# mLSTM heads of a hybrid recurrent decoder step: rows fetched one head ahead, exponents before the weight parts, own semaphores for three signals

## The chip, the cores and the metric

The kernel runs on one core of one Trainium2 chip. The metric is the device time of one execution in microseconds (us). The engines are named as in the profile: PE (TensorE), PEld (its weight loads), DVE (VectorE), ACT (ScalarE), POOL (GpSimd), SP (SyncE). SP and ACT issue the transfers (DMAs).

## The reference, cut to what matters

One step of a two-layer trunk runs for a prompt of 512 tokens and for 8 sampled sequences of 4 tokens each, with shared float32 weights. A layer is a SwiGLU block, a mixing block of three branches, and a second SwiGLU block. The change lies in the first two branches of the mixing block, of four heads each. Branch A is an mLSTM; per chunk:

```python
b = jnp.cumsum(fc, axis=-1)
D = jnp.where(causal, b[..., :, None] - b[..., None, :] + ic[..., None, :], -jnp.inf)
m_inter = b + m[..., None]
m_t = jnp.maximum(m_inter, jnp.max(D, axis=-1))
s_inter = jnp.exp(m_inter - m_t)
w = jnp.einsum('bhtd,bhsd->bhts', qc, kc) * jnp.exp(D - m_t[..., None])
num = jnp.einsum('bhts,bhsv->bhtv', w, vc) + s_inter[..., None] * jnp.einsum('bhvd,bhtd->bhtv', C, qc)
den = jnp.sum(w, axis=-1) + s_inter * jnp.einsum('bhd,bhtd->bht', n, qc)
h = num / jnp.maximum(jnp.abs(den), jnp.exp(-m_t))[..., None]
C_new = decay[..., None, None] * C + jnp.einsum('bhsv,bhsd->bhvd', vc * wk[..., None], kc)
```

The head's output goes through a layer norm and a gate. Branch B is a gated linear attention (GLA): `o = A v + (q exp(b)) S`, with a decay of each key dimension, an RMS norm and a gate. All final states are outputs too.

## The kernel before

The 544 tokens are the columns of every activation, features are the partitions. The prompt's chunks in the heads are 128 tokens long, four of them (`C`, `NC`); the 32 sample tokens are the columns from `T` on.

**The stream of weights.** Every projection is a sequence of blocks of weights, 1 MB each. SP loads a block into one of two halves of `stage` (`load`, L308) as soon as the block before in that half is split. A float32 weight is used in two parts: ACT writes the high part `wh` (`split_hi`, L729), DVE the rest `wl` (`split_lo`, L1002), and PE multiplies in three passes (`three_pass`, L379). A block gives two tiles of output, one in each pair of PSUM banks (`stream_a`, `stream_b`). DVE takes a tile out of PSUM (`take`, L992), which frees the pair. Every engine runs its own program in order, and semaphores tie them together: `split_done`, `hi_done`, `tile_done` and `tile_free` count blocks and tiles, others are those of a step.

**An mLSTM head** has four blocks and eight tiles: q (t), k (t+1), the values with tokens as rows (t+2 of the prompt, t+3 of the samples), two tiles of each of two gates (t+4 to t+7). Between them stands the head's own work, in four PSUM banks `mix` (`Q`). On PE (L505): q and k, values, then the scores and the transposed keys (L517 to L525, signal `a_scores`), tile t+4, the four updates of the state (`updates`, L535, which wait for `a_kw`), most of tile t+5, sample outputs, the outputs over the chunks (L553), tile t+6, the column sums of the mean (L573, wait for `a_h`, matmuls at L502), sample updates (L495), tile t+7, the column sums of the squares.

On ACT (L824) a head begins with the fetch of its row of four vectors of 544 numbers, spread over all partitions, out of a scratch tensor in DRAM (`RB`, L829). It then waits for it, makes `SI` and `EM` by exponentials (L832), waits for the stored states of the head before, loads `CS` and `nS`, makes two high parts, waits for `a_exin` from DVE and makes the exponents `Ex` (L842). Further on come the gates' sigmoids and `head_root`, a square root that ends the norm and for which GLA's next head waits (`root_done`, matmuls at L596).

On DVE (L1230): take q and k, split n+2, `qs`, take the values, among them `four_parts` of `V4` (L1157), split n+3, the two adds into `Ex` (L1249, L1252), signal `a_exin`, wait for `a_ex` and `a_scores`, then `wS`, `wSs`, `Kw` (the weighted keys for `updates`), `w1`, `Kf`, and `masked_keys` (L1170: four parts `K4`, then `Kws`, the operand of the sample updates), whose end is the one signal `a_kw`. Then `qn`, take t+4, the four states `Cst`, the merge of the head before, and so on. The denominators, the output `Hh`, its sum `wS` (L1294, signal `a_h`) follow the take of t+5 and split n+4.

Head 0 of a layer is a copy with `first=True`: its values are taken first, and the columns `cols` come out of PSUM before `a_exin`. Before it, `gate_rows` (L1106) builds the rows. On PE and DVE heads 1 to 3 are one loop; on ACT all four heads are.

**A GLA head** (PE L588, ACT L861, DVE L1309) has the same blocks. Its wait `b_took` of 10 releases its updates (L636); DVE signals it after `masked_keys`. Behind the states come the merge of the head before, take t+6, the copy out of `mix` (L1392), a square sum (L1210, signal `b_sqs`, which PE awaits at L657) and take t+7.

Of the kernel before, what the change touches and what calls it, by code (L numbers as in the profile page):

```python
# [23 lines left out]
ALU = mybir.AluOpType  # L24
ACT = mybir.ActivationFunctionType
ds = bass.ds
# [94 lines left out]
def trunk(nc, x_T, w_up1, w_down1, w_mix, w_gates, w_o, w_up2, w_down2, vec, b_if, w_lr2, w_ra, w_ri, consts, level_masks,  # L121
          m0, c0, n0, s0, h0, conv0, o_y, o_pc, o_pm, o_ps, o_ph, o_pconv,
          o_sc, o_sn, o_sm, o_ss, o_sh, o_sconv, rows_dram):
    with ExitStack() as ctx:
# [141 lines left out]
        a_mean, a_hc, a_sq, a_sqs = sem("a_mean"), sem("a_centred"), sem("a_squares"), sem("a_square_sum")  # L266
        a_var = sem("a_var")

        b_lr, b_cs = sem("b_lr_loaded"), sem("b_state_loaded")
# [108 lines left out]
        def _(pe):  # L378
# [126 lines left out]
            def mlstm_head(L, i, first=False):  # L505
# [20 lines left out]
                if first:  # L526
                    pe.wait_ge(rows_ready, L + 1)
                    for c in range(NC + 1):
                        row = merged[0:HEADS, 3, :]
                        m = C if c < NC else NS  # L530
                        mm = pe.matmul(Q[0:m, 2, 200 + c * HEADS:200 + (c + 1) * HEADS], row[:, c * C:c * C + m],
                                       ident[0:HEADS, 0:HEADS], start=True, stop=True)
# [40 lines left out]
                def mean():  # L573
                    pe.wait_ge(a_h, B + 1)
                    column_sum(wS, 0, a_mean)
                    sample_updates(0, 2, a_us)

# [10 lines left out]
            def gla_head(L, i):  # L588
# [49 lines left out]
                def outputs():  # L638
                    pe.wait_ge(b_c, B * NC + NC)
                    pe.wait_ge(b_cs, B * 16 + 16)  # L640
                    for v in range(2):
                        pe.matmul(Q[:, 2, v * NS:(v + 1) * NS], val[:, NC, v * P:(v + 1) * P], wSs[:],
                                  start=True, stop=False, skip_group_check=True)
                        sample_states(2, v, v * NS, lambda s_, v_: CS[:, s_, v_ * P:(v_ + 1) * P])
                    for v in range(2):
                        vs = slice(v * P, (v + 1) * P)
                        for c in range(NC):
                            sl = slice(c * C, (c + 1) * C)
                            mm = pe.matmul(Q[:, v, sl], val[:, c, vs], wS[:, sl], start=True, stop=c == 0)  # L649
                            if c:  # L650
                                mm = pe.matmul(Q[:, v, sl], Cst[:, c - 1, vs], qs[:, sl], start=False, stop=True)
                    mm.then_inc(b_out, 1)
                    sample_updates(0, 3, b_us)

# [62 lines left out]
        def _(act):  # L717
# [105 lines left out]

            def mlstm_head(L, i):  # L824
                B = L * HEADS + i
                nh = L * (LAYER_BLOCKS // 2) + i * (HEAD_BLOCKS // 2) + BLK_MIX // 2
                t = L * LAYER_TILES + i * HEAD_TILES + (TILE_MIX + GATE_TILES)
                stored = L * (16 * STORES) + i * 48 + 32
                act.dma_start(RB.rearrange("p a b -> p (a b)"),  # L829
                              spread(rows_dram[ds(i, 1), :], 0, P)).then_inc(a_rows, 16)  # L830
                act.wait_ge(a_rows, B * 16 + 16)
# [4 lines left out]
                act.dma_start(nS[:, 0, :], n0[L, i]).then_inc(a_cs, 16)  # L836
                split_hi(nh + 1, 0, t + 1, 2 * D)
                split_hi(nh + 1, 1, t + 3, 2 * D)
                act.wait_ge(a_exin, B + 1)
                for c in range(NC):  # L840
                    sl = slice(c * C, (c + 1) * C)
                    act.activation(Ex[:, sl], Ex[:, sl], ACT.Exp, bias=cols[:, ds(i + c * HEADS, 1)])  # L842
                act.activation(Ex[0:NS, T:N], Ex[0:NS, T:N], ACT.Exp,
                               bias=cols[0:NS, ds(i + NC * HEADS, 1)]).then_inc(a_ex, 1)
                gates = gate_tiles(t + 4)
                next(gates)
# [89 lines left out]
            def mix(L):  # L936
# [9 lines left out]
                act.dma_start(lr2[64:80, :], w_lr2[L, 0]).then_inc(b_lr, 16)  # L946
                with act.Fori(0, HEADS) as i:
                    mlstm_head(L, i)
                with act.Fori(0, HEADS - 1) as i:
                    gla_head(L, i)  # L950
# [32 lines left out]
        def _(dve):  # L983
# [122 lines left out]
            def gate_rows(L):  # L1106
# [11 lines left out]
                link(dve.tensor_tensor_scan(R[5], reset[0:HEADS, :], R[7], 0.0, ALU.mult, ALU.add))  # L1118
                link(tt_(R[3], R[4], R[5], ALU.subtract))
                take(L * LAYER_TILES + (TILE_MIX + GATE_TILES), 0, qT[:])  # L1120
# [31 lines left out]
            def take_sample_values(t):  # L1152
                tile_ready(t)
                v_ = val[0:NS, NC, 0:DV]
                ts_(v_, pair[1][C - NS:C, 0, 0:DV], rstdT[C - NS:C, NC:NC + 1], None, ALU.mult).then_inc(tile_free, 1)
                dve.wait_ge(tile_free, t + 3)
                four_parts(V4, v_, (0, 1), (2, 3))  # L1157

# [9 lines left out]
            def masked_keys(src):  # L1168

                four_parts(K4, src, (0, 2), (1, 3))  # L1170
                return tt_(Kws[:], spread(K4[:].bitcast(F32).unsqueeze(1), 1, SEQS), spread(seqm[:].unsqueeze(2), 2, P),
# [58 lines left out]
            def mlstm_head(L, i, first=False):  # L1230
# [7 lines left out]
                if not first:  # L1238
                    take(t, 0, qT[:])
                    take(t + 1, 1, kT[:], DK ** -0.5)  # L1240
                    split_lo(n + 2, 0, 2 * D)
                if first:
                    take_values(t + 2)
                dve.wait_ge(a_si, B + 1)
                link(tt_(qs[:], qT[:], SI, ALU.mult))
                if not first:
                    take_values(t + 2)
                split_lo(n + 3, 1, 2 * D)
                link(tt_(Ex[:, 0:T].rearrange("p (c t) -> p c t", c=NC),  # L1249
# [3 lines left out]
                if first:  # L1253
# [3 lines left out]
                    ins = dve.tensor_copy(cols[:, 0:NC * HEADS], Q[:, 2, 200:200 + NC * HEADS])  # L1257
                ins.then_inc(a_exin, 1)
                dve.wait_ge(a_ex, B + 1)
                dve.wait_ge(a_scores, B + 1)  # L1260
# [4 lines left out]
                link(tt_(wSs[0:NS], Ex[0:NS, T:N], Q[0:NS, 2, 0:NS], ALU.mult))  # L1265
                link(tt_(Kw[:], Q[:, 1, :].rearrange("p (c t) -> p c t", c=NC),
                         spread(exv[:, :, C - 1:C], 2, P), ALU.mult))
                link(dve.tensor_reduce(w1[0:NS], Ex[0:NS, T + TS - 1:N:TS], mybir.AxisListType.X, ALU.add))
                link(ts_(Kf[0:NS], Q[0:NS, 2, NS:NS + P], w1[0:NS], None, ALU.mult))
                masked_keys(Kf[0:NS]).then_inc(a_kw, 1)  # L1270


# [4 lines left out]
                for c in range(NC):  # L1277
                    states(c, DV + P, lambda c: SI[:, c * C + C - 1:(c + 1) * C], lambda c: c, a_u, a_c, B * NC)
                if not first:
                    merge_head(i - 1, True, number - 1)  # L1280
# [28 lines left out]
            def gla_head(L, i, first=False):  # L1309
# [72 lines left out]
                for e in range(NLS):  # L1382
                    link(dve.copy_predicated(As, masks[0:NS, NL - NLS + e, 0:NS], Q[0:NS, 1, (e + 1) * NS:(e + 2) * NS]))
                masked_keys(Q[0:NS, 1, P:2 * P]).then_inc(b_took, 1)
                take_gate(L, i, t + 5, 1, 1, acts + 1, "silu", None)
                split_lo(n + 4, 0, 2 * D)
                for c in range(NC):
                    states(c, DV, lambda c_: eb[:, c_ * C + C - 1:(c_ + 1) * C], lambda c_: c_, b_u, b_c, B * NC)
                merge_head(HEADS - 1 if first else i - 1, first, number - 1)
                take_gate(L, i, t + 6, 0, 0, acts + 2, "branch", gcol)  # L1390
# [277 lines left out]
```

## Time and profile before

| | us |
|---|---|
| median of 3 runs (range) | 3363.17 (3357.52 to 3373.01) |
| the profiled execution | 3364.34 |
| its span, first to last instruction | 3362.5 |
| PE busy in the span | 3217.6 |
| DVE busy | 1929.6 |
| ACT busy | 1011.5 |
| mean granted clock of TensorE | 0.972 of full speed |

Busy times are sums over all instructions of an engine. A row of a timeline gives the start and length of a group of like instructions that follow each other, and in brackets how long the engine idled before it and for whom. Rows of the window view give the granted clock as a share of full speed, which is 2.4 GHz; 0.50 is 1.2 GHz. Heads 0, 1, 2 and 3 of the first layer's mLSTM do their updates at 481.9, 556.7, 630.6 and 704.5 us of the span.

### The profile page before, as it was taken

What the parts mean: (1) busy time and instruction counts of PE and PEld (TensorE: products, weight loads), DVE (VectorE), ACT (ScalarE), POOL (GpSimd) and SP (SyncE); (2) the same over time, 40 slices, a digit from 0 to 9 for tenths busy, and PEclk for the clock granted to TensorE, in tenths of its full rate; (3) what the DMA queues carried; (4) which work ended last, traced back from release to release, by engine and by line L of the source; (5) the groups of instructions that cost most, each with busy time, mean ns of one, the idle gap of its engine ahead of it and who ended that gap; (6) DMA issues with size and microseconds to landing.
All of it is one profiled execution on the core that took longest, in us unless ns stands there. A gap on an engine that the chain in (4) does not pass through costs nothing.

```text
span 3362.5 us, 58957 instructions
## 1 busy us (share of the span) xinstructions
PE 3217.6 (96%) x24852; PEld 3163.4 (94%) x24852; DVE 1929.6 (57%) x2645; ACT 1011.5 (30%) x961; POOL 7.4 (0%) x24
## 2 busy tenths in 40 slices
PE   7999989999999999999999999899999999999997
PEld 7999989989999989999999999899899999899997
DVE  5434556657777875434454345555677778754344
ACT  3222222223332653212232123222333246432122
POOL 0000000000000000000000000000000000000000
PEclk9999989999999999999999999899999999999999
DMA  3222222232222222222222222133222222222222
GB/s 140 78 103 83 80 87 94 90 118 87 77 89 72 82 77 88 78 97 83 80 89 83 97 80 95 66 129 115 77 77 83 83 75 83 73 90 83 92 82 68
DMA packets 51744, 294.43 MB, mean 88 GB/s; under 512 B 9224, under 2 KB 12040, under 8 KB 22712
## 3 DMA queue, kind: packets, MB, share of 16 engines
q1 hardware_dynamic: 37440, 243.60, 21.2%
q10 hardware_dynamic: 13696, 48.54, 3.9%
q8 instruction: 68, 1.11, 0.1%
q0 software_dynamic: 512, 0.94, 0.1%
q14 instruction: 28, 0.23, 0.0%
HBM read 271.56 MB, written 21.50 MB: 87 GB/s over the span
## 4 chain that ended last, share of the span: by engine, by line
PE 75%; DVE 14%; ACT 6%; issue 4%; DMA 1%; ACTq 0%; DVEq 0%; SPq 0%
PE stream_b L383 33%; PE stream_a L383 29%; PE stream_a L457 5%; PE mix L487 2%; ACT wh L733 2%; DVE wl L1005 2%; PE mix L538 1%; DVE xc L1432 1%; PE mix L649 1%; PE mix L558 1%; DVE seven L1351 1%; DVE wS L1371 1%; ACT L919 1%; DVE tg L996 1%; PE stream_b L457 1%
## 5 line engine op out<-in xcount | busy, mean ns | idle before, releaser
L733 ACT ACTIVATE wh<-stage 128x2048 fp32r<-128x2048 f32 (+2 forms) x246 | 435.9, 1773 | 819.2 <-PE stream_b L383 586.9
L1005 DVE TENSOR_TENSOR wl<-stage,wh 128x2048 fp32r<-128x2048 f32 (+2 forms) x248 | 525.8, 2120 | 171.3 <-ACT wh L733 154.1
L383 PE MATMUL stream_a<-xh,wh 128*128 128x272 f32 x2560 | 545.6, 295 | 30.2 <-DVE wl L1005 16.1
L383 PE MATMUL stream_b<-xh,wh 128*128 128x272 f32 x2560 | 537.1, 291 | 9.3 <-DVE lyg L996 7.0
L383 PE MATMUL stream_a<-xh,wl 128*128 128x272 f32 x2560 | 536.4, 291 | 0.0
L383 PE MATMUL stream_a<-xl,wh 128*128 128x272 f32 x2560 | 535.0, 291 | 0.0
L383 PE MATMUL stream_b<-xh,wl 128*128 128x272 f32 x2560 | 528.5, 288 | 0.0
L383 PE MATMUL stream_b<-xl,wh 128*128 128x272 f32 x2560 | 528.1, 288 | 0.0
L383 PEld LDWEIGHTS stream_a<-xh,wh 128*128 128x128 f32 x2560 | 410.1, 192 | 37.6 <-issue 22.8
L383 PEld LDWEIGHTS stream_b<-xh,wh 128*128 128x128 f32 x2560 | 402.8, 188 | 15.1 <-DVE lyg L996 7.8
L383 PEld LDWEIGHTS stream_a<-xh,wl 128*128 128x128 f32 x2560 | 411.0, 192 | 0.0
L383 PEld LDWEIGHTS stream_a<-xl,wh 128*128 128x128 f32 x2560 | 407.8, 192 | 0.0
L383 PEld LDWEIGHTS stream_b<-xh,wl 128*128 128x128 f32 x2560 | 402.4, 189 | 0.0
L383 PEld LDWEIGHTS stream_b<-xl,wh 128*128 128x128 f32 x2560 | 400.3, 189 | 0.0
L996 DVE TENSOR_TENSOR us<-stream_b,rstd 128x544 f32<-128x544 f32 x88 | 63.8, 725 | 446.1 <-PE stream_b L383 445.9
L784 ACT ACTIVATE sg<-gs 128x544 f32<-128x544 f32 x88 | 58.0, 659 | 398.7 <-DVE gs L996 398.7
L457 PE MATMUL stream_a<-wh,xh 128*128 128x256 f32 x512 | 146.6, 286 | 6.1 <-DVE qT L996 6.1
L457 PE MATMUL stream_a<-wh,xl 128*128 128x256 f32 x512 | 147.2, 287 | 0.0
L383 PE MATMUL stream_b<-hh,wh 128*128 128x272 f32 x704 | 146.0, 289 | 0.0
L383 PE MATMUL stream_a<-hh,wh 128*128 128x272 f32 x704 | 146.0, 289 | 0.0
L457 PE MATMUL stream_a<-wl,xh 128*128 128x256 f32 x512 | 145.9, 285 | 0.0
L383 PE MATMUL stream_a<-hh,wl 128*128 128x272 f32 x704 | 145.3, 287 | 0.0
(325 smaller groups left out, 4684.9 us busy)
## 6 DMA issues: line engine op xcount, KB each, us to landing
stage<-in_w_up SPq DMA_DIRECT2D x88, 1024.0 KB, 4.8
stage<-in_w_mix SPq DMA_DIRECT2D x88, 1024.0 KB, 4.8
stage<-in_w_down SPq DMA_DIRECT2D x32, 768.0 KB, 4.2
stage<-in_w_down SPq DMA_DIRECT2D x32, 640.0 KB, 3.8
seven<-rows_scratch ACTq DMA_DIRECT2D x8, 1088.0 KB, 8.2
CS<-in_c ACTq DMA_DIRECT2D x8, 1024.0 KB, 4.7
out_o_sc<-CS ACTq DMA_DIRECT2D x8, 1024.0 KB
CS<-in_s ACTq DMA_DIRECT2D x8, 1024.0 KB, 4.8
```

The lines of the kernel that those rows point to most:

```text
L383: mm = [pe.matmul(out(h), a(h), b(h), start=f, stop=z) for h in range(2)]
L457: mm = pe.matmul(out, a[:, k, tok:tok + C], b[:, j, k * DV:(k + 1) * DV], start=f, stop=z)
L487: mm = pe.matmul(Q[:, b_, out_col + s_ * TS:out_col + (s_ + 1) * TS], lhs_of(s_, v), qs[:, T + s_ * TS:T + (s_ + 1) * TS], start=False, st ...
L538: pe.matmul(Q[:, c, 0:DV + P], Kw[:, c, :], val[:, c, :], start=True, stop=True).then_inc(a_u, 1)
L558: mm = pe.matmul(Q[:, v, sl], val[:, c, vs], wS[:, sl], start=True, stop=c == 0)
L649: mm = pe.matmul(Q[:, v, sl], val[:, c, vs], wS[:, sl], start=True, stop=c == 0)
L733: act.activation(wh[:, slot, 0:width], stage[:, slot, 0:width], ACT.Copy).then_inc(hi_done, 1)
L784: act.activation(sg[:], gs[:], ACT.Silu).then_inc(silu_done, 1)
L919: act.activation(lyg[:, v, :], lyg[:, v, :], ACT.Gelu_apprx_tanh).then_inc(l_act, 1)
L996: ins = tt_(halves(dst), banks(pair[slot]), rs2, ALU.mult)
L1005: tt_(wl[:, slot, 0:width], stage[:, slot, 0:width], wh[:, slot, 0:width].bitcast(F32), ALU.subtract).then_inc(split_done, 1)
L1351: tt_(ev[:, :, a, :], ev[:, :, a, :], sv[:, :, a, :], ALU.mult)
```

## The change

It has six parts. ACT fetches the rows of a head while the head before runs, behind that head's exponents (`load_rows`), and only the three rows in use. ACT's exponents of `Ex` stand ahead of the two high parts in heads 1 to 3; in head 0 between them; the heads of ACT are one copy for head 0, a loop of two, and one for head 3. DVE's adds into `Ex` stand right behind the take of k; split n+3 moves behind the states. `Kw` becomes the last step before `a_kw`; `masked_keys`, which now includes V4's parts, comes behind it and has its own signal `a_keys`. In GLA `masked_keys` moves behind the states, with a copy of the keys in its old place and a signal `b_keys` of its own. The wait in front of L531 is for a signal after row R[3] rather than for all rows.

```diff
@@ PE @@
                 if first:
-                    pe.wait_ge(rows_ready, L + 1)
+                    pe.wait_ge(a_row, L + 1)
...
                     column_sum(wS, 0, a_mean)
+                    pe.wait_ge(a_keys, B + 1)
                     sample_updates(0, 2, a_us)
...
                     mm.then_inc(b_out, 1)
+                    pe.wait_ge(b_keys, B + 1)
                     sample_updates(0, 3, b_us)
@@ ACT @@
+            def load_rows(i):
+                act.dma_start(RB[:, 0:3, :].rearrange("p a b -> p (a b)"),
+                              spread(rows_dram[ds(i, 1), 0:3 * N], 0, P)).then_inc(a_rows, 16)
...
-                act.dma_start(RB.rearrange("p a b -> p (a b)"),
-                              spread(rows_dram[ds(i, 1), :], 0, P)).then_inc(a_rows, 16)
                 act.wait_ge(a_rows, B * 16 + 16)
...
-                split_hi(nh + 1, 0, t + 1, 2 * D)
-                split_hi(nh + 1, 1, t + 3, 2 * D)
+                if first:
+                    split_hi(nh + 1, 0, t + 1, 2 * D)
                 act.wait_ge(a_exin, B + 1)
...
+                if not first:
+                    split_hi(nh + 1, 0, t + 1, 2 * D)
+                if not last:
+                    act.wait_ge(a_ex, B + 1)
+                    load_rows(i + 1)
+                split_hi(nh + 1, 1, t + 3, 2 * D)
                 gates = gate_tiles(t + 4)
...
-                with act.Fori(0, HEADS) as i:
+                load_rows(0)
+                mlstm_head(L, 0, first=True)
+                with act.Fori(1, HEADS - 1) as i:
                     mlstm_head(L, i)
+                mlstm_head(L, HEADS - 1, last=True)
@@ DVE @@
-                link(tt_(R[3], R[4], R[5], ALU.subtract))
+                tt_(R[3], R[4], R[5], ALU.subtract).then_inc(a_row, 1)
+                dve.wait_ge(a_row, L + 1)
...
                 dve.wait_ge(tile_free, t + 3)
-                four_parts(V4, v_, (0, 1), (2, 3))
...
+                four_parts(V4, val[0:NS, NC, 0:DV], (0, 1), (2, 3))
                 four_parts(K4, src, (0, 2), (1, 3))
...
                     take(t + 1, 1, kT[:], DK ** -0.5)
-                    split_lo(n + 2, 0, 2 * D)
...
                 dve.wait_ge(a_si, B + 1)
-                link(tt_(qs[:], qT[:], SI, ALU.mult))
-                if not first:
-                    take_values(t + 2)
-                split_lo(n + 3, 1, 2 * D)
...
                 ins.then_inc(a_exin, 1)
+                link(tt_(qs[:], qT[:], SI, ALU.mult))
+                if not first:
+                    split_lo(n + 2, 0, 2 * D)
+                    take_values(t + 2)
                 dve.wait_ge(a_ex, B + 1)
...
-                link(tt_(Kw[:], Q[:, 1, :].rearrange("p (c t) -> p c t", c=NC),
-                         spread(exv[:, :, C - 1:C], 2, P), ALU.mult))
...
-                masked_keys(Kf[0:NS]).then_inc(a_kw, 1)
+                tt_(Kw[:], Q[:, 1, :].rearrange("p (c t) -> p c t", c=NC),
+                    spread(exv[:, :, C - 1:C], 2, P), ALU.mult).then_inc(a_kw, 1)
+                dve.wait_ge(a_kw, B + 1)
+                masked_keys(Kf[0:NS]).then_inc(a_keys, 1)
+                dve.wait_ge(a_keys, B + 1)
...
                     states(c, DV + P, lambda c: SI[:, c * C + C - 1:(c + 1) * C], lambda c: c, a_u, a_c, B * NC)
+                split_lo(n + 3, 1, 2 * D)
@@ DVE, GLA head @@
-                masked_keys(Q[0:NS, 1, P:2 * P]).then_inc(b_took, 1)
+                dve.tensor_copy(Kf[0:NS], Q[0:NS, 1, P:2 * P]).then_inc(b_took, 1)
+                dve.wait_ge(b_took, B * 10 + 10)
...
                     states(c, DV, lambda c_: eb[:, c_ * C + C - 1:(c_ + 1) * C], lambda c_: c_, b_u, b_c, B * NC)
+                masked_keys(Kf[0:NS]).then_inc(b_keys, 1)
+                dve.wait_ge(b_keys, B + 1)
```

## Rows read from the trace of the kernel before

**Rows 1.** The page: span, and busy time, share and instructions of PE.
```profile
span 3362.5 us, 58957 instructions
PE 3217.6 (96%) x24852; PEld 3163.4 (94%) x24852; DVE 1929.6 (57%) x2645; ACT 1011.5 (30%) x961; POOL 7.4 (0%) x24
```

**Rows 2.** The waits of PE: for whom, us in total, times, longest.
```profile
PE mix L538 <- DVE Kws L1171: 31.6, 8, 4.7
PE mix L596 <- ACT hsq L821: 27.0, 8, 4.2
...
PE mix L502 <- DVE wS L1294: 0.6, 2, 0.3
```

**Rows 3.** Timeline of PE, mLSTM heads 0, 1 and 2: start, us, what, [idle before].
```profile
469.34 0.59 PE L383 MATMUL stream_a<-xh,wh 128*128 128x272 f32 x2 [2.90 <-DVE val L1148]
...
481.85 5.24 PE L538 MATMUL mix<-val,Kw 128*128 128x384 f32 x8 [4.72 <-DVE Kws L1171]
...
546.56 0.25 PE L525 MATMUL mix<-qT,kT 128*32 128x32 f32 x2
...
556.69 5.37 PE L538 MATMUL mix<-val,Kw 128*128 128x384 f32 x8 [3.68 <-DVE Kws L1171]
...
583.76 1.18 PE L502 MATMUL mix<-wS,ones 128*128 128x272 f32 x4 [0.29 <-DVE wS L1294]
...
630.61 4.26 PE L538 MATMUL mix<-val,Kw 128*128 128x384 f32 x8 [3.69 <-DVE Kws L1171]
```

**Rows 4.** Windows of PE: length, busy (x), granted clock, DMA share, GB/s.
```profile
500.00:504.00 4.00, 4.00 (x24) 0.57 0.45 147
...
556.70:561.40 4.70, 4.70 (x8) 0.50 0.00 0
...
720.00:724.00 4.00, 4.00 (x30) 0.78 0.11 14
```

**Rows 5.** Updates of mLSTM (all heads, by line) and of a GLA head (timeline).
```profile
L538 PE MATMUL mix<-val,Kw 128*128 128x384 f32 x64 | 37.2, 753 | 31.6 <-DVE Kws L1171 31.6
...
795.08 1.89 PE L636 MATMUL mix<-val,Kw 128*128 128x256 f32 x8
```

**Rows 6.** Timeline of DVE, mLSTM head 1.
```profile
545.24 0.49 DVE L1155 TENSOR_SCALAR val<-stream_b,rstdT 32x256 f32<-32x256 f32 x1 [1.64 <-PE stream_b L457]
...
547.34 2.29 DVE L1005 TENSOR_TENSOR wl<-stage,wh 128x2048 fp32r<-128x2048 f32 x1
549.55 0.69 DVE L1249 TENSOR_TENSOR seven<-seven,neg_p 128x512 f32<-128x512 f32 x1
...
552.10 0.69 DVE L1264 TENSOR_TENSOR wS<-seven,mix 128x512 f32<-128x512 f32 x1 [1.65 <-ACT seven L843]
...
553.95 0.34 DVE L1269 TENSOR_SCALAR Kf<-mix,w 32x128 f32<-32x128 f32 x1
...
555.41 1.23 DVE L1171 TENSOR_TENSOR Kws<-K,seqm 128x1024 fp32r<-128x1024 f32 x1
...
562.75 3.55 DVE L1217 RECIPROCAL hsq<-hsq 128x544 f32<-128x544 f32 x1
...
570.13 0.72 DVE L996 TENSOR_TENSOR tg<-stream_b,rstd 128x544 f32<-128x544 f32 x1 [2.36 <-PE stream_b L383]
```

**Rows 7.** ACT in heads 1 and 2, and the landing of the rows fetch (L829).
```profile
550.58 1.28 ACT L842 ACTIVATE seven<-seven,cols 128x128 f32<-128x128 f32 x4 [3.43 <-DVE seven L1252]
...
609.31 0.66 ACT L832 ACTIVATE seven<-seven 128x544 f32<-128x544 f32 x1 [6.73 <-DMA seven<-rows_scratch]
...
DMA to landing us min/median/max: 5.7/8.2/9.0
```

**Rows 8.** DVE in GLA: head 1's timeline, and waits before the copy, all heads.
```profile
891.37 1.22 DVE L1392 COPY Hh<-mix 128x1024 f32<-128x1024 f32 x1 [0.22 <-PE mix L651]
...
897.55 0.72 DVE L996 TENSOR_TENSOR tg<-stream_b,rstd 128x544 f32<-128x544 f32 x1 [2.85 <-PE stream_b L383]
...
DVE Hh L1392 <- PE mix L651: 5.2, 8, 2.0
```

More of the change, by code:

```diff
@@ L267, in trunk @@
         a_var = sem("a_var")
+        a_row, a_keys, b_keys = sem("a_exponent_row"), sem("a_sample_keys"), sem("b_sample_keys")
         b_lr, b_cs = sem("b_lr_loaded"), sem("b_state_loaded")
@@ L822, in head_root, with mlstm_head @@
                                scale=1.0 / DV).then_inc(root_done, 1)
-            def mlstm_head(L, i):
+            def load_rows(i):
+                act.dma_start(RB[:, 0:3, :].rearrange("p a b -> p (a b)"),
+                              spread(rows_dram[ds(i, 1), 0:3 * N], 0, P)).then_inc(a_rows, 16)
+            def mlstm_head(L, i, first=False, last=False):
                 B = L * HEADS + i
```

## The prediction, made before the changed kernel was run

> **What bounds the kernel now.** I read four views, in this order. The page: TensorE (PE) is busy for 3217.6 us of a span of 3362.5 [rows 1], no other engine for much more than half of it. So only time in which PE stands still, or runs at the lower of its two clock levels (2.4 and 1.2 GHz, 1.00 and 0.50 in the views), can be won. Second, whom PE waits for [rows 2]: the longest entry is the wait of the four update matmuls (L538) of an mLSTM head for `Kws` (L1171), 31.6 us in 8 waits, one a head. The next, 27.0 us at L596, is the gated-linear-attention (GLA) heads' wait for the previous head's root, which no line of the change shortens. Third, the timeline of PE in head 1 [rows 3]: scores end at 546.8, the tile t+4 runs, PE is ready at 553.01 (556.69 less 3.68) and the updates start at 556.69. The reader is to see that the eight records then last 5.37 us. The windows say why [rows 4]: the clock is at 0.50 in 556.7:561.4. The stall costs twice. Fourth, VectorE (DVE) in that stretch [rows 6]: its chain of work, and not a DMA, is what PE waits for.
>
> **Part 1, the wait for the weights of the updates.** Before, DVE does between the sample values (545.73) and the signal `a_kw` (556.64): V4's four parts, a 2.29 us split, the two adds into `Ex`, a wait for ScalarE's (ACT) exponents, `wS`, `wSs`, `Kw`, `Kf`, K4's parts and `Kws` [rows 6]. PE needs only `Kw` of it. Changed: the adds, 0.9 us from 549.55 [rows 6], and the exponents, 1.5 us from 550.58 [rows 7] to 552.10, stand behind the take of k, long before the scores, since the rows are there already. When the scores are out at 546.8 [rows 3], what is left is 552.10 to 554.29, with `Kw`'s 0.69 in it: 2.2 us [rows 6]. `a_kw` fires near 549.0, 4 us before PE wants it. Head 0 is tighter. There the adds and exponents follow the take of values; from PE's start on tile t+4 it is 0.5 (sample values), 0.9 (adds), 0.4 (two small copies into `cols`, an estimate), 1.5 (exponents), 2.2: 5.5 us, against 7.8 until PE is ready (469.34 to 481.85 less 4.72) [rows 3]. Both hide. **Term: -31.6 us**, bounds 0 and 31.6; I take all, as the margins are 4 and 2 us.
>
> **Part 2, the clock.** The 64 records of L538 take 37.2 us, 4.65 a head [rows 5]. GLA's L636 does the same work with 256 columns in place of 384, at full clock: 1.89 us for eight records [rows 5]. One record's tail is about 0.17, so 384 columns come to 1.72 * 1.5 + 0.17 = 2.75 us (estimate from that row). 37.2 - 8 * 2.75 = 15.2. **Term: -15.2 us**, bounds 0 (the drop comes at another place) and 17 (the first tile behind is slow too).
>
> **Part 3, the rows fetched ahead, three quarters of the bytes.** The fetch lands 5.7 to 9.0 us after its issue [rows 7]. In heads 1 to 3 this was in front of ACT's first weight part and now isn't; but PE shows no wait for that part there, so it is worth nothing by itself. ACT now sits at the wait for the stored states earlier, with the exponents behind it on its in-order queue, and DVE's split (n+2) behind those. The store's landing isn't shown; the rows fetch goes out behind it on the same queue and releases ACT at 609.31 [rows 7], which I take as its latest time. Then exponents (1.5), weight part (taken as long as DVE's, 2.3) and split (2.3) end by 615.4, and PE needs it behind its scores, at 546.8 + 630.61 - 556.69 = 620.7 [rows 3]. Cover 5 us, so nothing; if it were gone, each us late is a us, six times. The new fetch, behind the exponents, runs beside one load of weights that isn't needed before the next block. In head 0 the fetch is still in front of the first weight part, split and values, for which PE stalls 2.90 before 469.34 [rows 3]. A quarter of the bytes saves between 0 and 1.4 us (a quarter of 5.7); I take 0.7 a layer. **Term: -1.4 us.** The Trainium skill, page "DMA: Bandwidth & Descriptors", section "Anatomy of one DMA", gives 2.0 us plus the bytes over 436 GB/s, for the GpSimd path: by that estimate the whole fetch takes 4.6 us and the smaller one 3.9, the term would be -1.3 and the sum 0.1 us less of a gain; the 5.7 of the row is above it, and the row was used. The same page puts the longest completion on writes to HBM, which speaks against waiting for the store in front of the exponents; no row shows that landing.
>
> **Part 4, what DVE has to do later instead, mLSTM.** V4, K4 and `Kws` are now behind `a_kw`: 1.6 us (545.73 to 547.34) and 2.35 (554.29 to 556.64), 3.9 together [rows 6], and split n+3 is behind the states. Count for heads 1 to 3: 549.0 + 3.9 + 0.3 = 553.2; take of t+4 and sigmoid 1.5; four states 2.5: 557.2; split 2.3: 559.5; merge of the head before 5.0 (562.75 to 567.77): 564.5. PE has tile t+5 ready at 553.0 + 13.4 - 2.6 = 563.8 (13.4 is 556.69 to 570.1, 2.6 the clock's part). DVE is 0.7 late, where it idled 2.36 before [rows 6]. From there to the wait at L502 both chains are equally long in head 1: PE waited 0.29 there [rows 3]. In heads 2 and 3 there was no wait, [rows 2] lists 2 in all; PE lost time of its own to a drop of the clock with no stall before it, as in 720:724 or, in head 0, 500:504 (4 us at 0.57: 1.7 us lost) [rows 4], and that covers the 0.7. So 0.8 for one head of each layer, bounds 0 and 6 * 2.3 = 14 (the whole split in every head). **Term: +1.6 us.** The own semaphore `a_row` frees nothing: PE reaches L531 only behind the values and scores, long after either signal.
>
> **Part 5, GLA.** The parts V4, K4, `Kws` move to between the states and the merge: 3.9 us. Before the move they cost nothing (DVE then waits for PE's tile t+5 in every head), so nothing comes back. Behind it, DVE idled 0.22 before the copy at 891.37 and 2.85 before the take of t+7 [rows 8]. 3.9 - 0.22 - 2.85 = 0.8 late; that take starts the chain take, sigmoid, weight part, root, on which the next head's first matmul (L596) waits [rows 2]. Three heads of a layer; in its first one the idle before the copy is longest, 2.0 [rows 8], and swallows it. **Term: 6 * 0.8 = +4.9 us**, bounds 0 and 6 * 3.9 = 23.
>
> **Sum.** -31.6 - 15.2 - 1.4 + 1.6 + 4.9 = -41.7. The profiled execution took 3364.3 us, 1.2 above the median of 3363.2. 3364.3 - 41.7 = 3322.6; against the median 3321.5. I say 3322. About 0.5% (17 us) is what a measurement of this kernel can tell from no change.
>
> **Rivals.** (a) *The stall comes back smaller, further on.* DVE is late for `a_h` in all six heads by 0.8 to 2.3, and each such stall, with the small matmuls around it, brings a further drop of the clock like the one in 500:504 [rows 4], 1.7 us. For: the slack I count on in heads 2 and 3 is itself the product of a drop. Against: a drop on PE's path gives DVE back the slack it lacks, so the two hardly add up. Price 6 * (1.5 + 1.7) = 19, and 6 more in GLA: 3322 + 25 = 3347, about 3338 to 3353. (b) *The change doesn't remove the wait:* something else arrives last at the updates, ACT's exponents, because ACT is held by the stored-state wait or a weight part. Then PE waits as long as before and only Part 3 to 5 remain: 3364 + 5 = 3369, within 0.5%. Against: the margins of 4 and 5 us in Parts 1 and 3. (c) *Slower.* All DVE work that was moved lands uncovered, and each new stall drops the clock, at L502 and at the square-sum wait (L657). Price: eight mLSTM heads 3.9 + 2.3 + 1.7 = 7.9, eight GLA heads 3.9 + 1.7 = 5.6, 108 in all less 46.8 won less 1.4: 3364 + 60 = 3424; it decides for slower from 48 us, that is as soon as 45% of it comes true, 3 us a head on average. For it: the moved work, 6.2 us in an mLSTM head, is more than any idle there. Against: the idle of 2.36 and 2.85, and that DVE starts it 4 us earlier.
>
> **How the numbers follow.** Forecast 0.74, (a) 0.17, (b) 0.05, (c) 0.04. The forecast's own range: down to 3308 when Parts 4 and 5 cost nothing and some drops of the clock vanish with the stall (four at 1.7), up to 3336 with double costs in Parts 4 and 5 and some new drops. Stretched into most of (a), 3308 to 3346. Faster by over 0.5% means under 3346: the forecast and most of (a), 0.88. Same: a rest of (a) and (b), 0.08. Slower: (c), 0.04.
>
> **What would show it.** Right: no wait at L538 and its eight records in 2.7 to 2.9 us; clock 1.00 in them; `Kw` ending 4 us before them; `Kws` ending before L495; waits of about 1 us at L502 in head 1 and of 0.8 at L658 in GLA heads 1 to 3. Wrong: a wait on L842 or `Kw` at L538 (Part 1); low clock there without a wait (Part 2); stalls at L502 above 2 us in every head (Part 4).

## The result, and the profile after

The changed kernel takes 3322.05 us (median of 4 runs, 3320.92 to 3323.95) beside 3366.26 for the kernel before, ratio 0.988 with a 95% interval of 0.9867 to 0.9893. Predicted were 3322, in 3308 to 3346. The profiled execution has a span of 3322.2 us after one of 3362.5. The page of the changed kernel, to be read beside [rows 1]:

```profile
span 3322.2 us, 58852 instructions
PE 3208.6 (97%) x24852; PEld 3161.6 (95%) x24852; DVE 1930.4 (58%) x2653; ACT 1010.7 (30%) x961; POOL 7.4 (0%) x24
```

Work is the same; what is gone is idle PE (144.9 us before, 113.6 now) and PE time at the lower clock. The lines of the changed kernel are shifted: L539 is the update matmul (L538 before), L503 the column sum (L502), L496 the sample update (L495), L598 GLA's decay input (L596), L1187 `Kws`. The waits of PE (for whom, us in total, times, longest), beside [rows 2]:

```profile
PE mix L598 <- ACT hsq L824: 27.0, 8, 4.2
...
PE mix L503 <- DVE wS L1312: 5.9, 5, 1.9
...
PE mix L496 <- DVE hsq L1226: 2.7, 3, 0.9
...
PE stream_a L384 <- DVE val L1164: 2.1, 2, 1.1
```

The wait of 31.6 us at the updates is not in the list any more. Two small ones have grown or are new: the wait for `a_h` (L503), 0.6 before, and the one for GLA's square sum (`hsq`, L1226), of which the list of before had none. The update matmuls, by line and in head 2, beside [rows 3, 5]:

```profile
L539 PE MATMUL mix<-val,Kw 128*128 128x384 f32 x64 | 22.0, 486 | 0.0
...
612.08 2.74 PE L539 MATMUL mix<-val,Kw 128*128 128x384 f32 x8
```

That is 22.0 us for the 64 records after 37.2, 2.74 in a head where 2.75 was worked out. The window of the same matmuls, beside [rows 4], in the same columns but with all engines (PE, PEld, DVE, ACT, POOL):

```profile
612.00:614.80 2.80, 2.80 (x12) 1.74 (x12) 1.70 (x5) 0.66 (x1) 0.00 (x0) 1.00 0.00 0
```

The clock is 1.00 where it was 0.50. DVE's timeline in head 2, beside [rows 6]:

```profile
604.46 0.49 DVE L1171 TENSOR_SCALAR val<-stream_b,rstdT 32x256 f32<-32x256 f32 x1 [1.64 <-PE stream_b L458]
606.17 0.69 DVE L1279 TENSOR_TENSOR wS<-seven,mix 128x512 f32<-128x512 f32 x1 [1.22 <-PE mix L526]
...
607.67 0.69 DVE L1283 TENSOR_TENSOR Kw<-mix,seven 128x512 f32<-128x512 f32 x1
...
610.99 1.22 DVE L1187 TENSOR_TENSOR Kws<-K,seqm 128x1024 fp32r<-128x1024 f32 x1
...
617.00 2.29 DVE L1020 TENSOR_TENSOR wl<-stage,wh 128x2048 fp32r<-128x2048 f32 x1
619.21 3.54 DVE L1233 RECIPROCAL hsq<-hsq 128x544 f32<-128x544 f32 x1
...
624.35 0.72 DVE L1011 TENSOR_TENSOR tg<-stream_b,rstd 128x544 f32<-128x544 f32 x1
627.60 2.29 DVE L1020 TENSOR_TENSOR wl<-stage,wh 128x2048 fp32r<-128x2048 f32 x1 [2.52 <-ACT wh L736]
...
637.19 0.72 DVE L1312 TENSOR_TENSOR wS<-Hh 128x544 f32<-128x544 f32 x1
```

Three things are to be seen. DVE now waits 1.22 us for PE's scores and not for the exponents. `Kw` ends at 608.36, 3.7 us before the updates start. And the take of t+5 at 624.35 has no idle time before it, where there were 2.36 us. Between 606.17 and that take DVE idles only for parts of a us; the one longer wait behind it is for ACT's weight part, 2.52 us before 627.60. ACT at the start of head 3, beside [rows 7]: it doesn't wait for the rows when it makes `SI`, and the load of `CS`, which waits until the states of the head before are stored, goes out at 660.15. The last line is the landing of the rows fetch.

```profile
656.12 0.66 ACT L838 ACTIVATE seven<-seven 128x544 f32<-128x544 f32 x1
...
660.15 0.36 ACTq L841 DMA_DIRECT2D CS<-in_c  x1
...
DMA to landing us min/median/max: 3.9/4.2/5.5
```

**Where the time went, by heads.** I cut the trace at the first score matmul of each mLSTM head and the decay input of each GLA head. "Idle" is the length less PE's busy time; "slow" is (1 - clock) times the length, the time lost to the lower level (the clock is read to 0.01, so this is good to some 0.4 us). First layer, us, before and after:

| stretch | length | idle | slow |
|---|---|---|---|
| mLSTM head 0 to 1 | 81.5, 71.6 | 7.6, 1.4 | 6.5, 1.4 |
| 1 to 2 | 73.9, 68.9 | 4.0, 0.1 | 3.7, 1.4 |
| 2 to 3 | 73.9, 68.9 | 3.7, 0.1 | 3.7, 1.4 |
| 3 to GLA 0 | 52.2, 47.0 | 7.9, 5.9 | 3.7, 0.5 |
| GLA 0 to 3 (three heads) | 238.8, 241.1 | 12.7, 11.7 | 11.2, 16.1 |

Both layers: the mLSTM stretches are 561.8 us before and 514.8 after, 47.0 less; the GLA stretches 478.8 and 482.8, 4.0 more; the rest, which the change touches little, 2.6 more. Such a split of one trace is rough. In two runs below, the one with the GLA head as before and the one with the rows fetched at the head's start, the mLSTM stretches are 520.4 us long, 5.6 more than here, though the runs as a whole take as long as the changed kernel: where a drop of the clock falls, before or behind a cut, differs from run to run.

### The profile page after: what moved, and what is told of

It is laid out like the page before. It is cut to its first block, busy times and chain, and to the rows that moved or that the text cites. A ratio compares the mean times of both kernels' runs of the same rounds, so it can differ in the third digit from the quotient of the medians.

```text
span 3322.2 us, 58852 instructions
## 1 busy us (share of the span) xinstructions
PE 3208.6 (97%) x24852; PEld 3161.6 (95%) x24852; DVE 1930.4 (58%) x2653; ACT 1010.7 (30%) x961; POOL 7.4 (0%) x24
## 4 chain that ended last, share of the span: by engine, by line
PE 73%; DVE 15%; ACT 6%; issue 3%; DMA 1%; DVEq 0%; ACTq 0%; SPq 0%
PE stream_b L384 32%; PE stream_a L384 31%; PE stream_a L458 5%; ACT wh L736 2%; DVE wl L1020 2%; PE stream_b L458 1%; DVE hsq L1233 1%; DVE xc L1453 1%; PE mix L488 1%; DVE tg L1011 1%; DVE tg L1305 1%; DVE Cst L1209 1%; DVE wS L1389 1%; ACT L931 1%; DMA out_o_ss<-CS 1%
## 5 line engine op out<-in xcount | busy, mean ns | idle before, releaser
L384 PEld LDWEIGHTS stream_a<-xh,wh 128*128 128x128 f32 x2560 | 409.8, 192 | 35.0 <-issue 24.1
```

Of the source, the lines that this page charges most:

```text
L384: mm = [pe.matmul(out(h), a(h), b(h), start=f, stop=z) for h in range(2)]
```

## Experiments

All times are medians of four executions, beside six or seven of the kernel before on the same chip (medians 3362.5 to 3364.5).

### Which part brings the gain

**Updates wait for `Kws` again**, in the changed kernel:

```diff
-                    pe.wait_ge(a_kw, B + 1)
+                    pe.wait_ge(a_keys, B + 1)
```

> The changed kernel, but the updates wait again for the end of Kws, as before the change (Kw has no signal of its own for them). Theory (the gain comes from what was taken out in front of Kw: split n+3, V4's parts, the adds, the wait for the exponents): Kws ends about 3.9 us after Kw, at PE's own arrival, so PE waits 0 to 0.6 us a head and the time stays within 5 us of the changed kernel's 3322. Rival (the own signal is what does it): the wait of 3.7 us a head comes back with the low clock, 8 * 5.5 = 44 us, near 3364.

Measured: 3324.9 us, ratio 0.9886 (0.9869 to 0.9902), 2.9 us above the changed kernel. Its waits and update matmuls:

```profile
PE mix L539 <- DVE Kws L1187: 2.6, 2, 1.7
...
L539 PE MATMUL mix<-val,Kw 128*128 128x384 f32 x64 | 22.8, 499 | 2.8 <-DVE Kws L1187 2.6
```

Only the two heads 0 wait, 1.7 and 0.9 us, more than the 0.6 that was allowed for. The signal of its own is worth at most some 3 of the 44 us once the rest of the change is there, and with intervals that overlap even these aren't certain; the rival falls.

**Own signal alone**, in the kernel before (`Kw` last before `a_kw`, `masked_keys` behind it with `a_keys`, which PE awaits behind the column sum):

```diff
-                link(tt_(Kw[:], Q[:, 1, :]...
...
-                masked_keys(Kf[0:NS]).then_inc(a_kw, 1)
+                tt_(Kw[:], Q[:, 1, :]...).then_inc(a_kw, 1)
+                dve.wait_ge(a_kw, B + 1)
+                masked_keys(Kf[0:NS]).then_inc(a_keys, 1)
```

> The kernel before with one part of the change: Kw is the last step before a_kw and Kws has its own signal; V4's parts, split n+3, adds, exponents and rows stay. Theory: Kw ends 2.4 us earlier, a wait of 1.3 us a head is left of 3.7 (head 0: 2.3 of 4.7), 19 us of 31.6 won; if a wait that short still brings the low clock, the eight update records stay near 4.6 us a head and the time is 3345; if it doesn't, they take 2.75 and it is 3330. Rival (own signal does it all): 3322.

**Split n+3 moved alone**, in the kernel before:

```diff
-                split_lo(n + 3, 1, 2 * D)
                 link(tt_(Ex[:, 0:T]...
...
                     states(c, DV + P, ...)
+                split_lo(n + 3, 1, 2 * D)
```

> The kernel before with one other part of the change: split n+3 stands behind the states; signal, V4's parts, exponents and rows stay. Theory 1 (what counts is how much DVE does in front of the signal, whichever work it is): the signal comes 2.3 us earlier, a wait of 1.4 us is left in heads 1 to 3 and 2.4 in head 0, as with the own signal alone, and at such a length the eight update records stay at 2.8 us a head: 3340 to 3348. Rival (this move pays more, since head 0 needed it in the changed kernel): 3330.

Measured: 3343.6 (ratio 0.9938, 0.9921 to 0.9954) and 3340.4 (0.9930, 0.9911 to 0.9948): each alone brings half. The waits at the updates and the update matmuls, first of the own signal alone, then of the split alone:

```profile
PE mix L539 <- DVE Kw L1270: 11.2, 8, 1.8
...
L539 PE MATMUL mix<-val,Kw 128*128 128x384 f32 x64 | 22.8, 499 | 11.2 <-DVE Kw L1270 11.2
```
```profile
PE mix L538 <- DVE Kws L1171: 13.5, 8, 2.6
...
L538 PE MATMUL mix<-val,Kw 128*128 128x384 f32 x64 | 26.1, 556 | 13.5 <-DVE Kws L1171 13.5
```

The waits in heads 1 to 3 are what was worked out (1.3 and 1.4 us). In the heads 0 they are 1.8 and 1.3 us in the first run, where 2.3 was expected, and 2.5 and 2.6 in the second. With waits of up to 1.8 us the matmuls keep the full clock (22.8 in all, against 22.0 with no wait). The two waits of 2.5 and 2.6 us have slow matmuls behind them, which the expectation of 2.8 us a head had not; head 0 of the first layer:

```profile
478.03 4.54 PE L538 MATMUL mix<-val,Kw 128*128 128x384 f32 x8 [2.51 <-DVE Kws L1171]
```

My alternative of 3330 for "no low clock" was still wrong: the mLSTM heads then are 70.3 us long in the first run, with 2.9 us idle and nothing slow, against 68.9 in the changed kernel. At the updates 34.8 us are gone in the first run and 29.2 in the second, while the spans are only 22.9 and 24.1 us shorter. Part of it comes back at the wait for `a_h` (6.4 and 5.2 us after 0.6). Another part stands in the GLA heads, whose code is that of before: their stretches take 486.2 and 481.8 us after 478.8, with the same idle time and more low clock. Why the clock falls there more often is open.

**Split n+3 back in front of the scores**, in the changed kernel:

```diff
                     take_values(t + 2)
+                split_lo(n + 3, 1, 2 * D)
                 dve.wait_ge(a_ex, B + 1)
...
-                split_lo(n + 3, 1, 2 * D)
                 if not first:
                     merge_head(i - 1, True, number - 1)
```

> The changed kernel with split n+3 in front of the wait for the exponents again (behind the take of values), the rest as changed. Theory 1 (an mLSTM head is now as long as DVE's chain from the scores to the take of t+5; heads of 68.9 us in all of the first four runs, be it with 1.8 us of idle PE or with 1.4 us lost to the low clock): the split only changes its place in that chain, from behind the states to in front of Kw, where 1.2 us of idle are; Kw ends near 551.5 of the old frame, 1.5 us before PE; heads 68 to 69 us, time within 4 us of 3322. Rival (the move of the split is what removed the wait): wait at the updates of over 1 us a head, 3335.

Measured: 3334.9, ratio 0.9914 (0.9898 to 0.9931), 13 us above the changed kernel. That is the rival's time, but its wait of over 1 us a head came only in the two heads 0. PE in head 0 of either layer:

```profile
477.25 5.49 PE L539 MATMUL mix<-val,Kw 128*128 128x384 f32 x8 [3.98 <-DVE Kw L1284]
...
2124.84 4.31 PE L539 MATMUL mix<-val,Kw 128*128 128x384 f32 x8 [2.64 <-DVE Kw L1284]
```

and DVE in the first of them:

```profile
472.81 2.29 DVE L1020 TENSOR_TENSOR wl<-stage,wh 128x2048 fp32r<-128x2048 f32 x1 [3.38 <-ACT wh L736]
```

In head 0 the split waits 3.38 us for ACT's high part, which stands behind the exponents; PE waits 3.98 and its matmuls are slow again (5.49). In heads 1 to 3 no wait at the updates came, as theory 1 had it, but the stretches between their scores are 69.2 to 70.6 us long, 0.3 to 1.7 more. So the place of the split decides in head 0, together with the place of ACT's part, and costs little in the others: the theory had left head 0 out.

### The rows fetched ahead, and their size

**Rows fetched at the head's own start**, in the changed kernel:

```diff
+                load_rows(i)
                 act.wait_ge(a_rows, B * 16 + 16)
...
-                if not last:
-                    act.wait_ge(a_ex, B + 1)
-                    load_rows(i + 1)
...
-                load_rows(0)
```

> The changed kernel, but each head's rows (three of the four) are fetched at that head's own start, as before. Theory (the fetch ahead hides nothing that PE waits for): rows land near 8 us after their issue, adds, exponents, weight part and split follow and end 2 to 4 us before PE needs block n+2; no wait at the updates, 3322 to 3328. Rival (the fetch ahead is what brings the exponents in front of the scores): PE waits 2 to 4 us a head in heads 1 to 3 for split n+2 or for Kw, 6 * 4 with the clock, 3340 to 3350.

Measured: 3321.35, ratio 0.9872 (0.9856 to 0.9889): no difference to the changed kernel (3322.05), though the rows now land in 7.1 us (median). The fetch ahead, which gives the change its name, is worth nothing that can be measured.

**All four rows**, in the changed kernel:

```diff
-                act.dma_start(RB[:, 0:3, :]..., spread(rows_dram[ds(i, 1), 0:3 * N], 0, P))
+                act.dma_start(RB..., spread(rows_dram[ds(i, 1), :], 0, P))
```

> The changed kernel, but all four rows are fetched (1088 KB in place of 816). Theory 2 (the bytes count in head 0 alone, where first weight part, split and values stand behind the fetch): landing 1 to 1.5 us later, PE's wait before tile t+4 of head 0 longer by as much, twice a run: 3324 to 3326. Rival (the fetch's size is hidden in head 0 too): 3322.

Measured: 3324.2, ratio 0.9885 (0.9868 to 0.9903). Landing is 5.9 us (median) against 4.2 in the changed kernel and 4.2 to 4.9 in the other runs with three rows fetched ahead. The wait for the values before tile t+4 of head 0 is 8.2 us in all against 2.1, but other runs with three rows show 4.3 to 7.4. The 2.1 us between the medians point to theory 2 but lie within the intervals.

**ACT's first part of head 0 ahead of the wait for the rows**, in the version with both merges early (below):

```diff
+                if first:
+                    split_hi(nh + 1, 0, t + 1, 2 * D)
                 act.wait_ge(a_rows, B * 16 + 16)
...
-                if first:
-                    split_hi(nh + 1, 0, t + 1, 2 * D)
                 act.wait_ge(a_exin, B + 1)
```

> The version with both merges early (3307) and ACT's first weight part of head 0 in front of the wait for the rows. Theory 2 (what PE waits for in head 0, 2 to 4 us before tile t+4, is the weight part and split behind the rows fetch, so that a smaller fetch was worth its own shortening, about 1.5 us, and no more): the wait goes altogether, 3 us a layer with idle and low clock, 3301 (3298 to 3304). Rival (head 0 is bound by the values' take or the clock): 3307.

Measured: 3299.4, ratio 0.9807 (0.9790 to 0.9823), 7.7 us less than without it. The wait for the values is gone from PE's list. The stretch from head 0 to 1 is 69.6 and 68.7 us long, after 73.1 and 74.4: what stood in head 0 was the weight part behind the fetch.

### What bounds the heads now

**GLA head as before**, in the changed kernel (`four_parts` of V4 behind the values, K4 and `Kws` ahead of `b_took`, no `b_keys`):

```diff
-                dve.tensor_copy(Kf[0:NS], Q[0:NS, 1, P:2 * P]).then_inc(b_took, 1)
+                four_parts(K4, Q[0:NS, 1, P:2 * P], (0, 2), (1, 3))
+                tt_(Kws[:], ...).then_inc(b_took, 1)
...
-                masked_keys(Kf[0:NS]).then_inc(b_keys, 1)
```

> The changed kernel with the GLA head as it was (V4's parts with the values, K4 and Kws in front of b_took, no b_keys). Theory (moving 3.9 us between states and merge cost about 0.8 us a head in six heads, 4.9 forecast, 2.4 by the first trace's heads): 3317 to 3320, waits of PE on the square sum gone. Rival (the move in GLA is free, or a gain): 3322 or more.

Measured: 3321.4 (3317.5 to 3329.1), ratio 0.9879 (0.9862 to 0.9895). By the medians nothing, and neither expectation is decided. The wait for the square sum is gone as expected. The GLA stretches of the two layers are 480.0 us against 482.8, but that is no measure of the move. In all four profiles with the GLA head of before they are 478.8 to 486.2 us (mean 481.7); in the six with the head as changed 480.7 to 484.2 (mean 482.8). The difference is smaller than the spread that the low clock makes.

**The merge early in mLSTM heads, then in both**, in the changed kernel. The second adds the same in GLA, behind `b_zin`:

```diff
                 link(tt_(qs[:], qT[:], SI, ALU.mult))
                 if not first:
+                    merge_head(i - 1, True, number - 1)
                     split_lo(n + 2, 0, 2 * D)
...
-                if not first:
-                    merge_head(i - 1, True, number - 1)
```

> The changed kernel; in mLSTM heads 1 to 3 the merge of the head before (5.0 us of DVE) stands in DVE's idle time between k and the values instead of behind the states. Theory 1: DVE is no longer late at t+5, the heads shrink from 68.9 by up to the 1.8 us of idle or slow PE to 67.2 to 68.3: 3312 to 3319. Rival (the length of 68.9 is PE's own): no change, 3322.

> As the run before, and in GLA heads the merge stands right behind the first operation (decay input), in DVE's 5 to 6 us of idle there. Theory 1: masked keys no longer push the copy and the square sum, GLA heads end as early as before the change or earlier, 1 to 2.5 us a head less than in the changed kernel: 3298 to 3312. Rival (GLA heads are bound by PE and the root, so that nothing comes back): same as the run before.

Measured: 3315.4 (ratio 0.9856, 0.9840 to 0.9873) and 3307.2 (0.9838, 0.9821 to 0.9854). Theory 1 holds. Windows of PE from the scores of head 1 to those of head 2 (length, busy, clock, DMA share, GB/s), in turn of the changed kernel, of the one with the rows at the head's start, and of the one with the mLSTM merge early:

```profile
535.37:604.26 68.89, 68.76 (x533) 0.98 0.29 106
```
```profile
534.21:603.11 68.90, 67.14 (x533) 1.00 0.30 106
```
```profile
534.66:602.16 67.50, 67.21 (x533) 1.00 0.30 109
```

The first two are equally long, though one has 0.13 us of idle PE and a clock of 0.98, the other 1.76 us of idle at 1.00. DVE sets the length: if the clock drops, PE is slower and hardly waits; if not, it waits, 1.76 us here, for `a_h`. It isn't always one or the other. Of the 20 such stretches in the five builds that share this DVE chain 18 are 68.9 to 69.0 us long and two are 70.6, with 1.87 us of idle and a clock of 0.98 both (heads 2 to 3 of the second layer, in the runs with the rows at the head's start and with all four rows). With 5 us of DVE work taken out of that chain the head is shorter, whichever way it falls (67.5, or 68.5 with a drop).

**The decay input inside tile t**, on top of both early merges, and last with GLA's merge back and masked keys right behind the copy of the keys, together with ACT's first part as above:

```diff
-                pe.wait_ge(root_done, ...)      (and the two matmuls to b_z)
-                pair_block(n, t, 0)
+                pair_block(n, t, 0, None, (((6, decay_in),), ()))
```

```diff
                 dve.wait_ge(b_took, B * 10 + 10)
+                masked_keys(Kf[0:NS]).then_inc(b_keys, 1)
+                dve.wait_ge(b_keys, B + 1)
...
-                masked_keys(Kf[0:NS]).then_inc(b_keys, 1)
-                dve.wait_ge(b_keys, B + 1)
```

> As the run before, and PE does the GLA decay input matmuls (which wait 27.0 us in all for the previous head's root) after six of the eight parts of tile t instead of before it. Theory 1: the wait of 3.4 us a head and the low clock behind it (some 3 us a head lost in GLA heads) go, 8 * 5 = 40 us less, but DVE and ACT get the decay input 4 to 5 us later and had 2 us in hand before PE's scores, so 1 to 3 us a head come back: 3270 to 3290. Rival (the lateness comes back in full as a wait for the factors): 3305.

> The version with the decay input inside tile t and the mLSTM merge early, but in GLA the merge is back behind the states and masked keys stand right behind the copy of the keys, in DVE's 3.4 us of idle; and in head 0 ACT makes its first weight part before it waits for the rows. Theory 1 (in the earlier version the 6.3 us of merge at the head's start, and nothing else, make the prompt values late for PE, 14.6 us of waits): these waits fall to under 5 us and GLA heads from 78.5 to about 75 us; head 0 loses its 3 us wait twice: 3295 - 20 - 6 = 3269, range 3262 to 3280. Rival (the decay input itself is late): waits for values stay, 3290.

Measured: 3295.2 (ratio 0.9800, 0.9784 to 0.9816) and 3273.6 (0.9730, 0.9714 to 0.9746). The first came out above its range: the wait for the root is gone, but PE waits 14.6 us for the prompt values in its place. The second lies in its range. It brings that wait to 3.2 us and the three GLA heads of the first layer to 229.5 us from 233.5. Several edits are in it at once; only the one to ACT's first part has a run of its own, 7.7 us. It beats both kernels, the changed one by 48 us. PE's wait list of the last version, where the wait for the root no longer stands:

```profile
PE mix L646 <- DVE Cst L1211: 4.1, 6, 0.7
PE stream_a L384 <- DVE val L1166: 3.2, 4, 1.3
```

## Why the prediction was right, point by point

**Part 1, -31.6: right.** No wait at the updates. The margin of `Kw` is 3.7 us in head 2, 4 were forecast; in head 0 it is 0.5 (end at 473.28, updates at 473.79) where 2 were forecast. What the text didn't see is that `Kws` too would be ready in time: its own count had masked keys done at 553.2 and PE ready at 553.0. The first experiment shows it.

**Part 2, -15.2: right.** 37.2 us became 22.0. Shown also by lengths of the wait: 3.7 to 4.7 us (before, seven of eight heads), 2.5 and 2.6 (split alone), 2.6 and 3.98 (split back) have slow matmuls behind them; 0.9 to 1.8 (own signal alone, split alone in heads 1 to 3, updates on `Kws`) don't. A long wait doesn't always bring the low clock: in head 1 of the second layer of the kernel before the wait was as long as in its neighbours and the clock stayed at 1.00 (PE row; then the window, in the columns of the one above):

```profile
2219.18 2.85 PE L538 MATMUL mix<-val,Kw 128*128 128x384 f32 x8 [3.70 <-DVE Kws L1171]
```
```profile
2219.18:2222.10 2.92, 2.92 (x10) 1.86 (x11) 1.85 (x4) 0.66 (x1) 0.00 (x0) 1.00 0.00 0
```

**Part 3, -1.4: right in place and sign, the size uncertain.** The fetch lands in 4.2 us in head 0 after 5.7, but that is one trace. In seven profiles with three rows the first fetch of a layer takes 4.2 to 5.2 us (14 fetches, mean 4.7), in four profiles with four rows 5.7 to 6.0 (8 fetches, mean 5.8): 1.1 a layer, 2.2 in all, where I took 0.7 a layer as the middle of 0 and 1.4. The sentence from the Trainium skill, page "DMA: Bandwidth & Descriptors", section "Anatomy of one DMA", is for another path, and by its estimate the two sizes differ by 0.6 us; the runs here differ by 1.1. In the profiled executions the wait for the values fell by 4.1 us, but in other runs with the same fetch it was 4.3 to 7.4 us in all: PE comes to it later when the clock has fallen in the values' matmuls, as it had in the changed kernel's profile (0.66 in 445:455, and 1.00 there with the rows at the head's start). That the fetch ahead is worth nothing by itself was right. The store's landing, which the text had no row for, shows now: ACT's stores go out at 653.82 and 654.27 and release its next load at 660.15, 2.8 us after the exponentials for `SI` and `EM` have ended. PE's list has no wait for the weight part behind them in these heads.

**Part 4, +1.6: mis-sized, and in other heads.** Taking wait and slow matmuls away should have shortened head 1 by 3.68 + 2.63 = 6.3 us and head 2 by 3.69 + 1.52 = 5.2. They became 5.0 shorter each, so the cost is 1.3 in head 1 and 0.2 in head 2 (0.8 and 0 forecast), and near 0.2 in head 3: 1.7 in the first layer. In the second the same working gives 0.3, 0.3 and 2.9, so 5.3 in all where 1.6 were forecast. The sign named for it, a wait of about 1 us in head 1 of each layer, did not come: there it is nothing and 0.22 us. PE waits for `a_h` 1.75 us in head 3 of the first layer and 1.86 in heads 2 and 3 of the second, which the text held to be covered by a drop of the clock; only head 2 of the first was. With the rows fetched at the head's start the same wait is 1.76 or 1.88 us in five of the six heads 1 to 3. So DVE is some 1.8 us late in every such head when PE runs at full clock; the step had 0.7, and none in two heads of three.

**Part 5, +4.9: not confirmed.** (Six times 0.8 is 4.8.) The six stretches are 4.0 us longer, but that agreement is luck as far as the runs can tell: with the GLA code of before untouched they vary by 7.4 us from run to run, and the means of the two kinds of head differ by 1.1. The working fails too: head 0, which I had as free, became 2.0 us longer in the first layer, head 1 2.1, and head 2 1.8 shorter. The 0.8 us show as waits for the square sum only three times (2.7 us in all); the rest is low clock, which the step didn't have: idle fell by 1.0 us in the first layer and slow time rose by 4.9.

**Sum.** In the two profiles the mLSTM stretches lose 47.0 us (-31.6 - 15.2 - 1.4 + 1.6 = -46.6 forecast), the GLA stretches gain 4.0 and the rest 2.6; the spans differ by 40.3. By medians of the same measurement the gain is 44.2 us, from 3366.3, where the prediction started from 3363.2. The two large terms are shown. That the forecast and the median agree to 0.1 us is luck: three small terms are uncertain by several us, the starting value was 3 us off, and the four times of the changed kernel alone spread over 3 us. Of the rivals, (b) and (c) didn't occur. (a) did in part: the new waits exist (5.9 and 2.7 us), but in 18 of 20 stretches a wait and a drop of the clock take each other's place instead of adding up, which is what the text held against it.

## What to carry to other kernels

Before a signal is given earlier, count what the signalling engine does between its last real input and the signal; here it hardly mattered which piece was taken out (20.9 us for one, 22.1 for another), as long as no other engine was waited for instead, as in head 0. Then follow the pieces to where they land: here each was put in front of the next late take, and moving one more (the merge) into idle time was worth 14.9 us. A transfer that lands late is no wait until someone is seen waiting behind it.

## What the runs showed of the hardware that I had not expected

The low clock of PE can cost nothing where another engine sets the pace: heads of 68.89 us at a clock of 0.98 and of 68.90 at 1.00. And the rows fetch of 1088 KB lands in 8.2 us where it follows the store of a state on the same queue in six of eight heads, in 5.9 where it is fetched ahead, both by medians of eight; in the kernel before, the two fetches without a store ahead of them took 5.7 and 6.0. With three rows it is 7.1 and 4.2. No run changes the store alone, so that it is the cause is likely but not shown.
